# Scores and softmax of two attention waves begun during the value projection, and two w_ada chunks in halves between later waves

## What is computed

```python
sc = jax.nn.silu(c)
mod = sc @ w_ada[i] + b_ada[i]                      # 1024 x 6144
sh_m, sc_m, g_m, sh_f, sc_f, g_f = jnp.split(mod, 6, axis=-1)
h = modulate(x, norm_mix[i], sh_m, sc_m)
y = moba_attention(h, w_qkv[j], w_o[j], ...)        # first layer
x = x + g_m[:, None, :] * y
h = modulate(x, norm_ffn[i], sh_f, sc_f)
x = x + g_f[:, None, :] * swiglu(h, w_gate_up[i], w_down[i])

def moba_attention(h, w_qkv, w_o, q_gain, k_gain):
    qkv = h @ w_qkv                                 # 3 x 8 heads x 128
    q = rms_norm(qkv[0], q_gain) * (HEAD_DIM ** -0.5)
    k = rms_norm(qkv[1], k_gain)
    # one block of 256 keys: causal softmax attention over 256 tokens
    p = jax.nn.softmax(masked(q @ k.T), axis=-1)
    return (p @ qkv[2]) @ w_o
```

## Time and profile before

| | |
|---|---|
| three timed runs | 1751.18, 1751.7, 1752.1 us; median 1751.7 us |
| the profiled execution | 1752.87 us, of which the span is 1751.2 us |
| busy in the span | PE 1420.7 us (81%), DVE 1076.2 (61%), ACT 774.2 (44%), POOL 94.8 (5%) |
| DMA | 327.64 MB, 187 GB/s on average |
| chain that ended last, by engine | PE 64%, DVE 21%, ACT 10%, issue 3%, DMA 1% |

### The profile page before, as it was taken

One profiled execution on the slowest core, in us unless ns is written; L12 is line 12 of the kernel. 1 busy time (PEld: TensorE's weight loads), 2 busy tenths in 40 slices (PEclk: granted clock), 3 DMA queues, 4 the chain that ended last, 5 costly groups with the idle time before them and its releaser, 6 DMA issues.

```text
span 1751.2 us, 19084 instructions
## 1 busy us (share of the span) xinstructions
PE 1420.7 (81%) x7190; PEld 1199.2 (68%) x7190; DVE 1076.2 (61%) x1061; ACT 774.2 (44%) x757; POOL 94.8 (5%) x96
## 2 busy tenths in 40 slices
PE   4985899998977999789775768888877675888884
PEld 4964788877966888588764656666677455666663
DVE  7683587876747654534594466776654327576775
ACT  3653434343334344334532336565535434375552
POOL 0010000000000000000032020000030002000000
PEclk8997899998989999899867779999889786899998
DMA  9982389985555555434501228787646010588870
GB/s 363 351 289 98 100 285 306 304 276 201 185 168 176 185 191 187 148 117 149 168 1 37 72 96 286 260 277 261 237 130 209 1 48 29 186 274 279 278 251 24
DMA packets 205880, 327.64 MB, mean 187 GB/s; under 512 B 9504, under 2 KB 140256, under 8 KB 205808
## 3 DMA queue, kind: packets, MB, share of 16 engines
q1 hardware_dynamic: 192512, 276.71, 47.3%
q0 software_dynamic: 13296, 49.93, 8.5%
HBM read 325.56 MB, written 1.05 MB: 187 GB/s over the span
## 4 chain that ended last, share of the span: by engine, by line
PE 64%; DVE 21%; ACT 10%; issue 3%; DMA 1%; SPq 0%; DVEq 0%; ACTq 0%
PE ps L1821 19%; PE ps L1823 19%; PE ps L1822 19%; DVE w_low L1132 7%; ACT w_high L620 5%; DVE scratch L1538 1%; PE ps L2321 1%; DVE scratch L1520 1%; DVE scratch L1178 1%; PE ps L1892 1%; DVE small L1732 1%; PE ps L2020 1%; PE ps L2066 1%; ACT small L999 1%; PE ps L2007 1%
## 5 line engine op out<-in xcount | busy, mean ns | idle before, releaser
L1132 DVE TENSOR_TENSOR w_low<-raw,w_high 128x2048 fp32r<-128x2048 f32 (+1 forms) x256 | 580.6, 2272 | 419.8 <-ACT w_high L620 417.8
L620 ACT ACTIVATE w_high<-raw 128x2048 fp32r<-128x2048 f32 (+1 forms) x256 | 483.9, 1893 | 487.9 <-PE ps L1823 460.8
L1821 PE MATMUL ps<-w_high,h_high 128*128 128x512 f32 (+1 forms) x928 | 376.0, 405 | 41.6 <-DVE h_low L1726 18.5
L1823 PE MATMUL ps<-w_high,h_low 128*128 128x512 f32 (+1 forms) x928 | 368.3, 397 | 0.0
L1822 PE MATMUL ps<-w_low,h_high 128*128 128x512 f32 (+1 forms) x928 | 368.0, 397 | 0.0
L1821 PEld LDWEIGHTS ps<-w_high,h_high 128*128 128x128 f32 x928 | 183.4, 198 | 81.1 <-DVE h_low L1726 19.4
L1823 PEld LDWEIGHTS ps<-w_high,h_low 128*128 128x128 f32 x928 | 182.4, 197 | 38.1
L1822 PEld LDWEIGHTS ps<-w_low,h_high 128*128 128x128 f32 x928 | 183.4, 198 | 35.2 <-issue 0.2
L1821 PE MATMUL ps<-h_high,w_high 128*128 128x256 f32 x624 | 183.7, 294 | 19.0 <-DVE h_low L1225 13.4
L1822 PE MATMUL ps<-h_low,w_high 128*128 128x256 f32 x624 | 181.7, 291 | 0.0
L1823 PE MATMUL ps<-h_high,w_low 128*128 128x256 f32 x624 | 181.4, 291 | 0.0
(11 more groups left out here) (308 smaller groups left out, 1512.1 us busy)
## 6 DMA issues: line engine op xcount, KB each, us to landing
raw<-in_w_down SPq DMA_DIRECT2D x124, 512.0 KB, 4.3
raw<-in_w_gate_up SPq DMA_DIRECT2D x88, 512.0 KB, 4.9
scratch<-in_w_ada POOLq DMA_DIRECT2D x40, 1024.0 KB, 5.6
raw<-in_w_gate SPq DMA_DIRECT2D x80, 512.0 KB, 4.0
raw<-in_w_up SPq DMA_DIRECT2D x80, 512.0 KB, 5.1
raw<-in_w_qkv SPq DMA_DIRECT2D x24, 512.0 KB, 13.1
raw<-in_w_o SPq DMA_DIRECT2D x24, 512.0 KB, 5.8
raw<-in_w_in SPq DMA_DIRECT2D x24, 512.0 KB, 4.9
```

The costliest lines, as they stand in the source:

```text
L620: act.activation(wh[u % SPL][:, :, 0:w], raw[u % RAW][:, :, 0:w], ACT.Copy).then_inc(h_split, 1)
L1132: dve.tensor_tensor(wl[u % SPL][:, :, 0:w], raw[u % RAW][:, :, 0:w], wh[u % SPL][:, :, 0:w].bitcast(F32), ALU.subtract).then_inc(l_split, 1)
L1821: pe.matmul(o, h1, h2, start=start, stop=False, skip_group_check=True)
L1823: return pe.matmul(o, l1, h2, start=False, stop=stop, skip_group_check=True)
```

## The change

The scores and maxima of waves 0 and 1 and their Exp move from behind the value projection into its two chunks, and the division of wave 0 with them; for that the first attention gets other banks: scores in 6, 7 (even waves) and 4, 5 (odd waves), transposes in 0, 1, outputs in 2 and 3. PE computes the scores of wave 0 between chunks 4 and 5, and those of wave 1 between the two units of chunk 5. The `ada` of chunks 8 and 9 leaves chunks 4 and 5; a half of a chunk now stands at the end of each step i = 2, 3, 4, 5 of the wave loop on DVE. The split of unit 14 moves on both engines into step 2. The work as such is the same: each engine has as many instructions as before.

```diff
+        LATE_BANKS = dict(scores=(0, 2), turned=4, outs=6)
+        EARLY_BANKS = dict(scores=(6, 4), turned=0, outs=2)
...
ACT
             for c in range(6):
+                if c == 5:
+                    ahead(PLAN["qkv"] + 10)
+                    exps(MOBA, EARLY_BANKS, 1)
                 chunk_ready("qkv", c)
...
                     act.activation(tv[:, :, (c - 4) * NC:(c - 3) * NC], pair(), ACT.Copy).then_inc(lin_evac, 1)
                     act.wait_ge(lin_evac, evac.up())
+                    if c == 4:
+                        exps(MOBA, EARLY_BANKS, 0)
                 lin[0] += 1
-            ahead(PLAN["wo0"])
...
+            heads(MOBA, EARLY_BANKS, 2, lambda i: i == 2 and ahead(PLAN["wo0"]))
...
DVE
             for c in range(6):
+                if c == 5:
+                    probs(MOBA, 0)
+                    maxima(MOBA, EARLY_BANKS, 1)
                 ahead(PLAN["qkv"] + 2 * c + 1)
...
                 if c == 4:
                     dve.wait_ge(row_loaded, 32)
                     mod_gate(0, 6)
-                ada(0, 4 + c, acc_of(0, 4 + c))
-            ahead(PLAN["wo0"])
+                    maxima(MOBA, EARLY_BANKS, 0)
+                if c < 4:
+                    ada(0, 4 + c, acc_of(0, 4 + c))
+
+            def ada_between(i):
+
+                ada(0, 8 + (i - 2) // 2, acc_of(0, 8 + (i - 2) // 2), parts=(i % 2,))
+                if i == 2:
+                    ahead(PLAN["wo0"])
+
+            heads(MOBA, EARLY_BANKS, 2, ada_between)
...
PE
-            for c in range(6):
-                chunk("features" if c < 4 else "rows", fresh=c == 0)
...
+            def second_scores():
+
+                pe.wait_ge(rs_ready, rsr.up())
+                scores(MOBA, EARLY_BANKS, 1)
+
+            for c in range(6):
+                chunk("features" if c < 4 else "rows", fresh=c == 0, between=second_scores if c == 5 else None)
...
+                if c == 4:
+                    pe.wait_ge(mod_taken, mtk.up())
+                    pe.wait_ge(masks_loaded, 48)
+                    pe.wait_ge(normed, nrm.up(3))
+                    scores(MOBA, EARLY_BANKS, 0)
+            pe.wait_ge(lin_evac, 6)
+            pe.wait_ge(normed, nrm.up())
+            heads(MOBA, EARLY_BANKS, 2)
```

More of the change, by code:

```diff
@@ new lines, in heads @@
+            def heads(waves, banks, begun=0, between=None):
+                for i in range(begun, len(waves) + 2):
+                    if i < len(waves):
+                        maxima(waves, banks, i)
+                    if 0 <= i - 1 < len(waves):
+                        probs(waves, i - 1)
+                    if i >= 2:
+                        m = waves[i - 2]
+                        b = slice(m["blk"], m["blk"] + m["nb"])
+                        head_low(out_of(i - 2, m, banks), hh[:, b, :], hl[:, b, :])
+                    if between:
+                        between(i)
@@ L1306, in heads @@
[L1306 to L1336, removed]
@@ L1858, in _, with chunk @@
             lin = [0]
-            def chunk(kind, w=NC, fresh=False):
+            def chunk(kind, w=NC, fresh=False, between=None):
                 if lin[0] >= 2:
@@ L1872, in chunk @@
                     n[0] += 1
+                    if between and q == 0:
+                        between()
                 lin[0] += 1
@@ L1964, in square_sums, with scores, heads @@
                 sqs.up()
-            for c in range(6):
-                chunk("features" if c < 4 else "rows", fresh=c == 0)
[L1968 to L1981, removed]
             sr, er, pr = Count(s_ready), Count(e_ready), Count(p_ready)
             ptr, pte, orr = Count(pt_ready), Count(pt_evac), Count(o_ready)
[L1987 to L1999, removed]
+            def scores(waves, banks, w):
+                if w >= 2:
+                    pe.wait_ge(e_ready, er.up())
+                for a, m in enumerate(waves[w]["heads"]):
+                    bank = score_banks(w, banks)[:, a, :]
+                    for c0, c1, x, y in m["scores"]:
+                        i = pe.matmul(bank[:, c0:c1], x, y, start=True, stop=not m["masked"], skip_group_check=True)
+                        if m["masked"]:
+                            i = pe.matmul(bank[:, c1 - P:c1], ident[:, :], mcausal[:, :], start=False, stop=True,
+                                          skip_group_check=True)
+                i.then_inc(s_ready, 1)
+                sr.up()
+            def heads(waves, banks, begun=0):
                 def turn(w):
@@ L2006, in turn @@
                         for x, y in waves[w]["turns"]:
[L2007 removed]
+                            i = pe.transpose(ps[:, banks["turned"] + a, y:y + P], prob(w)[:, a, x:x + P], ident[:, :])
                     i.then_inc(pt_ready, 1)
@@ L2023, in outs @@
                     orr.up()
-                for i in range(len(waves) + 2):
-                    if i < len(waves):
-                        scores(i)
+                for i in range(1 if begun else 0, len(waves) + 2):
+                    if begun <= i < len(waves):
+                        scores(waves, banks, i)
                     if 0 <= i - 1 < len(waves):
```

102 lines of the change are left out of this document (83 added, 19 removed).

## The result

The changed kernel is slower: 1757.72 us median of six timed runs (1756.59 to 1760.39), against 1751.9 of six of the kernel before. The ratio is 1.0032, 95% interval 1.0022 to 1.0042, so 3.9 to 7.4 us (0.3%) more. The profiled execution took 1756.59 us, its span is 1754.9 us; the span of before was 1751.2, so this pair differs by 3.7 us.

The account below looks back on a forecast made before the run. DVE bounds the stretch before the first transposes, a PE-DVE-ACT chain the waves, PE the output projection; -7.3 + 2.2 + 9.7 - 2.7 - 0.5 + 1.7 + 2.0 = +5.1 on 1751.7 gives 1756.8 us, range 1752 to 1761.5.

Parts of the forecast that it names:

- Step 1: Ahead of chunk 5: PE waits for DVE's gate before the scores of wave 0, standing still for 7.4 us.
- Step 2 and 3: From the gate to the first transposes: 7.3 us sooner at full clock, 2.2 us lost to half clock after the stall.
- Step 4: Between the waves: the ada halves delay DVE's critical work by 4.1, 3.1, 2.5 and 0 us, +9.7 in all.
- Step 5: PE's clock in the attention and at the output projection: terms of -2.7, -0.5, +1.7 and +2.0 us.
- The sum: All terms together: +5.1 us, with the output projection ending near 197 rather than 192 us.
- Behind it: After the output projection: norm and feed-forward follow in a chain, so nothing gives the 5.1 us back.
- the later dips: Later in the kernel: clock dips fall anew, each restart losing 1 to 3 us either way; 3 us allowed in the range.
- the clock stays up: Rival: granted clock at 1.00 throughout the changed place, sum -3.1, 1748.6 us; 27% together with in-between cases.
- the halves fit in: Rival: the ada halves hide in DVE's waits between the waves, sum -4.5, 1747.2 us; 5%.
- nothing starts early: Rival: the first transposes come no earlier and only the costs remain, 1764 us; 3%.

Follow-up runs that it names:

- e1: The changed kernel with DVE taking the attention gate (mod_gate) in chunk 3 instead of chunk 4; ratio 0.9992 against the kernel before.
- e4: The changed kernel with eight extra, unused matmuls on PE in the stall ahead of the scores of wave 0; ratio 1.0028 against the kernel before.
- e3: The kernel before with only the halves of ada 8 and 9 between the waves and unit 14 split in step 2, scores late; ratio 1.0007 against before.
- e7: The changed kernel with chunk 9 of ada behind the last h_low and chunk 8 left between the waves; ratio 1.0010 against the kernel before.
- e2: The changed kernel with all four ada halves behind the last h_low, under the output projection; ratio 0.9989 against the kernel before.
- e5: The kernel before with ada 8 and 9 behind the last h_low and unit 14 split in step 2, scores late; 1746.49 us, ratio 0.9952 against before.
- e6: The changed kernel with the gate taken in chunk 3 and all four ada halves behind the last h_low; 1743.27 us, ratio 0.9942 against before.
- e8: The changed kernel with the split of unit 14 moved behind the last wave on DVE and ACT; ratio 1.0026 against the kernel before.

## Why the prediction was right, point by point

The time of 1757.72 us lies in the range and 0.9 us above the forecast of 1756.8, and it is slower by more than 3.5 us, as was held likeliest. That it came so close is in part luck: the timed difference is known only to 3.9 to 7.4 us, and the two profiles differ by 3.7. What speaks for the mechanism is that its terms were found one by one.

- **Step 1**, the new wait: 7.4 us forecast, 7.48 measured, ended by the gate at 116.81. Right, and e1 shows that it was on the path.
- **Step 2 and 3**, the way to the first transposes: 16.9 us and 2.2 for the clock were forecast from 116.75. It took 19.7 (116.81 to 136.50), so the clock cost 2.8, near the upper bound, which is also what e4 gives back there. The transposes came at 136.50 where the prediction's terms give 135.85. The granted clock fell and returned as expected; the windows of the changed kernel:

```profile
112.00:113.00 1.00, 0.00 (x0) 0.00 (x0) 0.00 (x0) 1.00 (x1) 0.00 (x0) 0.89 0.91 351
...
122.00:123.00 1.00, 1.00 (x4) 0.71 (x4) 0.69 (x1) 0.20 (x1) 0.00 (x0) 0.50 0.00 0
123.00:124.00 1.00, 1.00 (x6) 0.84 (x5) 0.00 (x0) 0.93 (x5) 0.00 (x0) 0.99 0.00 0
```

  One reading in step 2 was loose: I put the gain of the removed `ada` at 7.3 us and called the rest eaten by the wait. e3 gives the two apart: 12.1 us from the `ada` and, at the first transposes, 7.6 lost by the early scores with their wait and their half clock. I had named the loss but not asked whether the part "scores earlier" brought anything at all. It didn't.
- **Step 4**, the halves: 4.1, 3.1, 2.5 and 0 us. Measured: the maxima of wave 3 began 3.6 us after its scores had ended (148.34 to 151.90), before 0.1 us after them (155.55 to 155.66), so 3.5; the division of wave 3 began 3.2 us after `h_low` ended (160.08 to 163.26), before 0.03, so 3.1; `h_low` of wave 3 lost 2.3, by e7. Sum 8.9 instead of 9.7. The first came out smaller in part because half clock had made those scores longer (3.3 us from 145.07, before 2.7 from 152.86). The fourth cost nothing: behind it DVE was idle for 6.40 us. The second has no run of its own and rests on these rows.
- **Step 5**, the clock in the waves: transposes 0 and scores 2 took 3.1 us (136.50 to 139.58), as forecast. Transposes 2 and outputs 1 took 4.1 us (154.49 to 158.59), forecast 3.9. The waves as a whole took 36.8 us, by my terms 37.3. The projection lost 1.6 us (23.5 instead of 21.9) for 2.0 forecast, with the half clock not at its start but from 174 to 178 us.
- **The sum**: +5.1 us at the end of the projection, measured +4.8 (192.03 and 196.83).
- **Behind it** I saw nothing that gives anything back. That was wrong by 1.3 us in the profile: the feed-forward began 4.80 us later (210.05, before 205.25), but with the clock already up, where before it ran at half clock until the window of 208 us. ACT's table load in it comes at 217.79 against 214.32, so the lag is 3.5 there, and 3.7 at the end of the span. It lies within the 3 us that I had put on the later dips.

PE's first feed-forward matmuls, changed kernel:

```profile
210.05 0.47 PE L1847 MATMUL ps<-w_high,h_high 128*128 128x512 f32 x1 [1.41 <-DVE h_low L1238]
210.36 0.39 PE L1848 MATMUL ps<-w_low,h_high 128*128 128x512 f32 x1
```

- **The rivals**: that the clock stays up is out by the windows, that the halves fit in is out by e2, and that nothing starts early is out by the transposes of wave 0, 4.5 us sooner than before.

## What to carry to other kernels

Before moving work into the idle time of an in-order engine, ask of each insertion who waits for the instruction right behind it: here DVE was idle for 20 of 29 us, and yet 8.9 of the 14.3 us inserted (four halves of about 3.0 and a split of 2.29) came out as lateness. The halves behind the last step of the chain, under a stage that PE alone fills, left no gap on PE (e2), and that move by itself (e5) gained 10.3 us of the place where the whole change lost 4.8. An early start is only as early as its latest input: the scores moved forward had to wait for banks that DVE freed only behind the last `qk_norm`, though e1 shows that they can be freed a chunk earlier, and everything that PE could have done instead stood behind them.

## What the runs showed of the hardware

The same instructions of a late stretch, which no edit touches, took 97.0 us in two profiles and 100.3 in a third, with a lower granted clock in the third. The stretch lies between two ACT table loads in the second block, at 1348.30 and 1445.27 us before. The windows of before, of the changed kernel and of e7:

```profile
1348.30:1445.30 97.00, 61.82 (x298) 47.71 (x296) 33.33 (x40) 38.85 (x57) 0.00 (x0) 0.81 0.10 34
```

```profile
1351.90:1448.90 97.00, 61.81 (x298) 47.68 (x296) 33.35 (x40) 38.87 (x57) 0.00 (x0) 0.81 0.11 34
```

```profile
1349.90:1450.20 100.30, 65.96 (x299) 50.86 (x296) 33.32 (x39) 38.85 (x57) 0.00 (x0) 0.76 0.10 32
```

DVE and ACT are busy for the same time to 0.03 us; PE is busy for 4.1 us longer, at a mean clock of 0.76 instead of 0.81. Between the same loads e2, e3 and e6 took 96.9 to 97.0 us as well, and e1, e4, e8 and e5 took 99.4, 99.5, 99.7 and 100.2. So a shift of a few us in one place is not simply carried to the end; it meets other clock falls. Which ones does not follow from the size of the shift alone: e7's stretch began between those of before and of the changed kernel. The single span of one profile is no measure of an effect of 3 us. Part of the spread between runs of one kernel is probably this (before: 1749.99 to 1757.72 us in 23 runs), which no run here isolates.

The moment at which the clock rises isn't fixed by the program either. The same instructions, untouched by any edit, began within 0.03 us of each other, after some 6 us of idleness, and saw the clock rise at different times. PE's timeline and windows of before, and then of e3:

```profile
39.79 0.55 PE L1821 MATMUL ps<-h_high,w_high 128*128 128x256 f32 x1 [6.01 <-DVE h_low L1225]
```

```profile
43.00:44.00 1.00, 1.00 (x7) 1.00 (x7) 1.00 (x1) 1.00 (x1) 0.00 (x0) 0.50 1.03 399
44.00:45.00 1.00, 1.00 (x9) 1.00 (x9) 1.00 (x1) 0.63 (x1) 0.00 (x0) 0.85 1.05 399
```

```profile
39.76 0.55 PE L1830 MATMUL ps<-h_high,w_high 128*128 128x256 f32 x1 [5.61 <-DVE h_low L1225]
```

```profile
43.00:44.00 1.00, 1.00 (x9) 1.00 (x9) 1.00 (x1) 1.00 (x1) 0.00 (x0) 0.76 1.04 404
```

In before the whole window of 43 us is at 0.50 and the rise falls into the next one; in e3 it falls into the window of 43 us. By the mean clock of these windows that is 0.8 us apart. The Trainium skill ("TensorE: Matmul & The Clock Gate", Part 1), which the prediction used for this, says that the chip's rhythm doesn't reset with a kernel. These 0.8 us agree with it; that there is a rhythm at all is not shown by two rises.
